# The last block of a convolutional MLP computed by feature tile in two banks, and a mean square issued between two products

## The reference

```python
mixed = jnp.sum(gates * proj, axis=2) @ w_out[l]
x = x + _rms_norm(mixed, norm_mix_post[l])
...                                   # cross attention: ox
x = x + _rms_norm(ox, norm_x_post[l])

hf = _rms_norm(x, norm_ffn_pre[l])
u = _dwconv_causal(hf @ w_up[l], ffn_dw[l]) + ffn_dw_b[l]
u_g, u_v = jnp.split(u, 2, axis=-1)
yff = (jax.nn.silu(u_g) * u_v) @ w_down[l]
x = x + _rms_norm(yff, norm_ffn_post[l])
```

## Time and profile before

| | |
|---|---|
| median of 3 runs | 1330.28 us (1328.29 to 1332.39) |
| the profiled execution | 1330.64 us |
| its span (first to last instruction) | 1328.5 us |
| PE busy | 1282.4 us (97%) |
| DVE busy | 838.8 us (63%) |
| ACT busy | 672.4 us (51%) |
| POOL busy | 57.7 us (4%) |
| granted TensorE clock, mean | 0.99 of full speed |
| read from HBM | 209.14 MB, 158 GB/s |

### The profile page before, as it was taken

How to read it: one execution, slowest core, us unless ns; L and a number is a source line. 1 busy time by engine, 2 the same in 40 slices (tenths; PEclk the granted TensorE clock), 3 DMA queues, 4 the chain that set the end, 5 groups by cost and what they waited for, 6 DMA issues and landing times.

```text
span 1328.5 us, 22392 instructions
## 1 busy us (share of the span) xinstructions
PE 1282.4 (97%) x9224; PEld 1201.5 (90%) x9224; DVE 838.8 (63%) x1129; ACT 672.4 (51%) x925; POOL 57.7 (4%) x101
## 2 busy tenths in 40 slices
PE   5999998999999999999999999899999998999997
PEld 5999997999999998899999999888999987999996
DVE  4874447655555655655555589986556566766664
ACT  4874656544445454444444554645354445654552
POOL 4000002000000000100000000010000010000000
PEclk8999999999999999999999999899999999999999
DMA  7750104555554644455654655444556642555550
GB/s 238 203 164 28 64 1 156 193 191 188 189 189 159 206 159 159 147 187 189 189 189 158 211 171 159 128 127 128 159 152 198 190 157 68 177 189 189 189 189 32
DMA packets 160465, 211.32 MB, mean 159 GB/s; under 512 B 5541, under 2 KB 143219, under 8 KB 160387
## 3 DMA queue, kind: packets, MB, share of 16 engines
q1 hardware_dynamic: 157299, 202.77, 48.0%
q0 software_dynamic: 2048, 7.37, 1.6%
q10 hardware_dynamic: 1040, 0.07, 0.1%
HBM read 209.14 MB, written 1.05 MB: 158 GB/s over the span
## 4 chain that ended last, share of the span: by engine, by line
PE 80%; DVE 11%; ACT 4%; issue 2%; DMA 2%; POOL 1%; DVEq 0%; SPq 0%; POOLq 0%; ACTq 0%
PE bank L306 23%; PE bank L309 23%; PE bank L310 23%; PE bank L1173 5%; DVE wlo L300 3%; DVE common L2198 2%; ACT whi L292 1%; PE bank L1662 1%; PE bank L1180 1%; ACT common L544 1%; DVE xlo L615 1%; DMA raw<-in_dn_w_in 1%; PE bank L2218 1%; PE bank L1744 1%; PE bank L1785 1%
## 5 line engine op out<-in xcount | busy, mean ns | idle before, releaser
L300 DVE TENSOR_TENSOR wlo<-raw,whi 128x2048 fp32r<-128x2048 f32 x191 | 437.1, 2291 | 248.4 <-ACT whi L292 248.0
L306 PE MATMUL bank<-xhi,whi 128*128 128x256 f32 x1824 | 523.5, 287 | 12.3 <-DVE xlo L615 11.4
L309 PE MATMUL bank<-xlo,whi 128*128 128x256 f32 x1824 | 516.9, 283 | 0.0
L310 PE MATMUL bank<-xhi,wlo 128*128 128x256 f32 x1824 | 516.9, 283 | 0.0
L292 ACT ACTIVATE whi<-raw 128x2048 fp32r<-128x2048 f32 x191 | 364.4, 1910 | 176.4 <-PE bank L306 107.2
L306 PEld LDWEIGHTS bank<-xhi,whi 128*128 128x128 f32 x1824 | 350.9, 192 | 18.1 <-issue 13.8
L309 PEld LDWEIGHTS bank<-xlo,whi 128*128 128x128 f32 x1824 | 350.8, 192 | 2.6 <-issue 1.0
L310 PEld LDWEIGHTS bank<-xhi,wlo 128*128 128x128 f32 x1824 | 350.6, 192 | 0.0
L306 PE MATMUL bank<-whi,hhi 128*128 128x512 f32 x392 | 154.0, 393 | 3.4 <-DVE hlo L2647 2.5
L309 PE MATMUL bank<-wlo,hhi 128*128 128x512 f32 x392 | 153.7, 392 | 0.0
L310 PE MATMUL bank<-whi,hlo 128*128 128x512 f32 x392 | 153.1, 390 | 0.0
(11 more groups left out here) (318 smaller groups left out, 1572.5 us busy)
## 6 DMA issues: line engine op xcount, KB each, us to landing
raw<-in_mlp_w_up SPq DMA_DIRECT2D x32, 1024.0 KB, 5.4
raw<-in_mlp_w_down SPq DMA_DIRECT2D x32, 1024.0 KB, 5.0
raw<-in_w_in SPq DMA_DIRECT2D x22, 1024.0 KB, 5.3
raw<-in_w_up SPq DMA_DIRECT2D x22, 1024.0 KB, 5.1
raw<-in_dn_w_in SPq DMA_DIRECT2D x16, 1024.0 KB, 6.1
raw<-in_w_gate SPq DMA_DIRECT2D x16, 1024.0 KB, 5.7
raw<-in_mb_w_in SPq DMA_DIRECT2D x12, 1024.0 KB, 5.1
raw<-in_w_down SPq DMA_DIRECT2D x11, 1024.0 KB, 4.8
```

The costliest lines, as they stand in the source:

```text
L300: nc.vector.tensor_tensor(wlo[:, s, :], raw[:, V % RAW, :], f32(whi[:, s, :]), ALU.subtract).then_inc(lo_ready, 1)
L306: ins = pe.matmul(o, shi, mhi, start=first, stop=False, skip_group_check=True)
L309: pe.matmul(o, shi, mlo, start=False, stop=False, skip_group_check=True)
L310: return pe.matmul(o, slo, mhi, start=False, stop=last, skip_group_check=True)
```

## The change

The last block (10) is computed differently from the other ten. Its gate half stays as it is. In its value half feature tile 0 goes to bank `G[1]` and feature tile 1 to bank `G[2]`, and each has its own signal when it is full. ScalarE applies silu ahead of the value half's first taps. First tap, other taps, product, `hhi` and `hlo` are then done for each feature tile on 256 columns. The order on ScalarE is first tap 0, first tap 1, `hhi` 0, `hhi` 1; on VectorE taps and product 0, taps and product 1, `hlo` 0, `hlo` 1. TensorE's last product waits for `hlo` 0 ahead of block 10's first feature tile (k = 0) and for `hlo` 1 ahead of its second (k = 1), in token tile 0 only. In `add_normed_rows` the mean square stands between the two products with the gains instead of behind them; this holds for all three places that use it.

```diff
-        def gemm_rows_by_tile(pe, Us, uses, operands, ready, first=False, between=None):
+        def gemm_rows_by_tile(pe, Us, uses, operands, ready, first=False, between=None, late=None):
...
                     for k in range(2):
+                        if late and t == 0 and n == len(Us) - 1:
+                            pe.wait_ge(late[k].sem, late[k].value)
                         for c in range(2):
...
                 for k in range(2):
                     use, squared = uses[2 * t + k], r.ss[2 * t + k]
+                    if k:
+                        dve_mean_square(dve, r, t)
                     dve.wait_ge(squared.sem, squared.value)
                     nc.vector.tensor_tensor(norm_x[:, t, HALF[k]], use.ps[:, :], gain_buf(g)[:, HALF[k]], ALU.mult)\
                         .then_inc(use.freed, 1)
-                dve_mean_square(dve, r, t)
...
+            z = tb[-1]
+            z_uses = [z.uses[1], G[2 + z.p].use() if z.p == 0 else G[0].use()]
+            z_y, z_mid, z_pr, z_hi, z_lo = (Signal(sem(f"ffn_last_{n_}")).many(2)
+                                            for n_ in ("first_tap", "mid", "prod", "hi", "lo"))
+            z_ft = z.ft + FF // P
+
+            def z_part(ap, f):
+                return ap[:, f * T:(f + 1) * T]
+
+            def pe_last(pe):
+                gemm_features(pe, z.us[0], z.uses[0], xhi, xlo)
+                sl_ = z.us[1] % RING
+                pe.wait_ge(lo_ready, z.us[1] + 1)
+                wh, wl = wview(whi, sl_, KT), wview(wlo, sl_, KT)
+                for f in range(2):
+                    if z_uses[f].n:
+                        pe.wait_ge(z_uses[f].freed, z_uses[f].n)
+                    fs = slice(f * P, (f + 1) * P)
+                    for k in range(KT):
+                        ins = mm3(pe, z_part(z_uses[f].ps, f), wh[:, k, fs], wl[:, k, fs], xhi[:, k, :], xlo[:, k, :],
+                                  k == 0, k == KT - 1, f == 0 and k == 0)
+                    ins.then_inc(z_uses[f].filled, 1)
+
+            def act_last(act):
+                act_half(act, z, 0, 0)
+                act_block(act, z, 0)
+                for f in range(2):
+                    act.wait_ge(z_uses[f].filled, z_uses[f].n + 1)
+                    nc.scalar.activation(z_part(cg[2 + z.p], f), z_part(z_uses[f].ps, f), ACT.Identity,
+                                         scale=w_ap(2, z_ft + f), bias=b_ap(z_ft + f)).then_inc(z_y[f].sem, 1)
+                for f in range(2):
+                    act.wait_ge(z_pr[f].sem, z_pr[f].value)
+                    nc.scalar.activation(hhi[:, z.p, f, :], z_part(prod[z.p], f), ACT.Copy).then_inc(z_hi[f].sem, 1)
+
+            def dve_last_taps(dve, f):
+                dve.wait_ge(z_y[f].sem, z_y[f].value)
+                dst = z_part(cg[2 + z.p], f)
+                for tap, sh in ((1, 1), (0, 2)):
+                    if tap == 0:
+                        dve.wait_ge(z_mid[f].sem, z_mid[f].value)
+                    ins = nc.vector.scalar_tensor_tensor(dst[:, sh:], z_part(z_uses[f].ps, f)[:, 0:T - sh],
+                                                         w_ap(tap, z_ft + f), dst[:, sh:], ALU.mult, ALU.add)
+                    ins.then_inc(z_mid[f].sem if tap else z_uses[f].freed, 1)
+                dve.wait_ge(z_uses[f].freed, z_uses[f].n + 1)
+                dve.wait_ge(z.sl.sem, z.sl.value)
+                nc.vector.tensor_tensor(z_part(prod[z.p], f), z_part(cg[z.p], f), dst, ALU.mult)\
+                    .then_inc(z_pr[f].sem, 1)
+
+            def dve_last_lo(dve, f):
+                dve.wait_ge(z_hi[f].sem, z_hi[f].value)
+                nc.vector.tensor_tensor(hlo[:, z.p, f, :], z_part(prod[z.p], f), f32(hhi[:, z.p, f, :]), ALU.subtract)\
+                    .then_inc(z_lo[f].sem, 1)
+
+            def dve_last(dve):
+                dve_half(dve, z, 0, 0)
+                dve_last_taps(dve, 0)
+                dve_last_taps(dve, 1)
+                dve_last_lo(dve, 0)
+                dve_last_lo(dve, 1)
...
                 gemm_rows_by_tile(pe, [td[-1], dl], acc, [(hhi[:, q], hlo[:, q]) for q in qs],
-                                  [[(prev[0], prev[1] + tail - 1)], [(prev[0], prev[1] + tail)]])
+                                  [[(prev[0], prev[1] + tail - 1)], []], late=z_lo)
```

More of the change, by code:

```diff
@@ L2700, in pe_f @@
                 for k in range(tail):
-                    pe_block(pe, tb[k])
+                    if k == tail - 1:
+                        pe_last(pe)
+                    else:
+                        pe_block(pe, tb[k])
                     q = (k + 1) % 2
@@ L2731, in act_f @@
                         act_all(act, lb[k], L[3 * k + 2], 12, i)
-                for k in range(tail):
+                for k in range(tail - 1):
                     act_all(act, tb[k], td[k], 0)
-                split_hi(act, dl)
+                act_last(act)
             def dve_f(dve):
@@ L2741, in dve_f @@
                         dve_all(dve, lb[k], L[3 * k + 2], 12, i)
-                for k in range(tail):
+                for k in range(tail - 1):
                     dve_all(dve, tb[k], td[k], 0)
-                split_lo(dve, dl)
+                dve_last(dve)
             return Part(pe=pe_f, act=act_f, dve=dve_f, acc=acc)
```

## The result

The changed kernel takes 1325.0 us (median of 5, 1323.55 to 1326.65), the kernel before 1332.16 us in the same comparison. The ratio is 0.995, with a 95% interval of 0.993 to 0.9969: between 4.1 and 9.3 us less, where 5.9 were forecast. The profiled execution took 1324.11 us, 6.5 less than the one before.

The account below looks back on a forecast made before the run. TensorE was taken to carry 80% of the chain, so less idle time or a shorter chain it waits for pays: 2.5 + 1.64 + 1.8 = 5.9 us less, 1324.3 us against the median, range 1322.3 to 1327.5.

Parts of the forecast that it names:

- The hole: TensorE's 2.62 us idle time between block 9's and block 10's rows in the last product: forecast to shrink by 2.5.
- Rival C: Last block: `hlo` of tile 0 comes late behind tile 1's product; hole 0.6 us, 1324.8 us; chance 0.05.
- rival E: Last block: the change doesn't take hold, tile 0's chain slides into tile 1's; 1325.8 us; chance 0.05.
- The clock: TensorE's matmuls behind the hole: without it no fall of the granted clock, 1.64 us less.
- rival A: Last product: TensorE's clock falls all the same, costing 1.64 us; 1326.0 us; chance 0.16.
- Rival D: Last product: without its hole TensorE stays at the low clock for all 48 matmuls; 1333.9 us; chance 0.04.
- The hand-overs and the tail: Behind mixer, cross attention and last product: earlier mean square gains 0.6 us in each hand-over, 0.62 in the tail.
- Rival B: Hand-overs and tail: POOL's root is blocked by VectorE's second product, taking 0.99 instead of 0.55; 1325.9 us; chance 0.08.
- one row of waits: Behind the hand-over's update, squares, root, transposes, split and TensorE's restart wait in a row, so the 0.6 gain is kept.
- low end: Whole kernel: upper bounds of all terms, 6.3 us, and 1.6 more should the clock's fall near 1104 vanish; 1322.3 us.
- the fall at 1104: TensorE's granted clock of 0.61 over 1104 to 1108; might vanish with the shifted hand-over, 1.6 us more gain.

Follow-up runs that it names:

- x8: Changed kernel, VectorE reordered: tile 1's update before tile 0's norm half in hand-overs, `hlo` 0 before product 1 in last block; ratio 0.9965 to kernel before.
- x10: Changed kernel with the last block's signals from existing semaphores and `hlo` of tile 0 ahead of tile 1's product; 1325.21 us, ratio 0.9951 to kernel before.
- x3: Kernel before, with ten spare TensorE products into an unused bank while it waits ahead of block 10; ratio 0.9984 to the kernel before.
- x5: Changed kernel with one bank for both feature tiles, signalled once, VectorE waiting for both first taps; ratio 0.9965 to the kernel before.
- x6: Kernel before, with an unused 512-column VectorE product beside POOL's root in the tail: one bank operand in tile 0, two buffers in tile 1; 1330.9 us.
- x1: Changed kernel with the mean square put back behind both products, so only the last block is changed; ratio 0.9968 to the kernel before.
- x7: Kernel before with only the last block's silu moved ahead of the value half's first taps on ScalarE; 1332.6 us, one run.
- x9: Kernel before with five more semaphores that nobody uses; 1331.05 us, one run.

## Why the prediction was right

**The hole.** Forecast 2.5 less (2.62 to 0.1); 2.62 to 0.00, with 0.08 in the first step behind it. The chain of small pieces was right to some hundredths: product and split at 0.42, `hlo` of tile 0 as the last thing to come, TensorE just at its own end when it comes. This is why x8's and x10's earlier `hlo` could gain only 0.08. Rival C needed small products and splits of 0.70, and they took 0.42; rival E needed tile 0's chain to slide into tile 1's, and tile 0's product ends at 1305.02, 0.91 before tile 1's taps begin.

**The clock.** Forecast 1.64 less; 9.66 - 8.02 = 1.64. That the hole is its cause was argued in the prediction from its place alone, and rival A stood against it; x3 shows it. In x5's one profile a hole of 1.8 us did no harm there. Rival D fell with the rows of the changed kernel: no matmul of the last product is at 0.43.

**The hand-overs and the tail.** Forecast 0.6 each and 0.62; they gave 0.63 and 0.64 (8.88 to 8.25 and 8.90 to 8.26) and 0.60. Rival B needed a root of 0.99 beside the second product; it took 0.55, and x6 shows both cases in one kernel. The prediction took all that stands behind the update as one row of waits; x8 shows a second path, that of tile 0's half. The change did not run into it, because that half keeps its place, 1.36 us behind the product before and after.

**The sum.** 2.62 + 1.64 + 0.63 + 0.64 + 0.60 = 6.13 us in the profile, forecast 5.9. One count in the prediction is off without touching the sum: ScalarE issues one instruction more, not two (its page has 926 beside 925, VectorE's 1131 beside 1129). The median came out at 1325.0 where 1324.3 was forecast, and the kernel before took 1.9 us more in this comparison than the median from which the forecast started. The timed gain of 4.1 to 9.3 us holds the forecast 5.9 but is too wide to test its terms; the rows do that. The profiled executions differ by 6.53; the rest is in places that the change doesn't touch: 1.56 less in the cross attention, where the clock did not fall this time, 1.05 more up to the first hand-over, 0.11 more behind the last update. The prediction's low end counted the fall at 1104 as something that a shorter hand-over might remove. It does not: x1 lacks the fall with the old hand-over, x5 and x8 have it with the new one. It comes and goes from profile to profile and is worth 1.3 to 1.6 us each time (31.15 to 31.43 beside 29.87). How much of the spread of the timed runs it makes up was not measured.

## What to carry to other kernels

Where the last chain behind a product decides when the next product starts, split it so that its first half runs under the producer's second half. Here smaller instructions with a wait for each tile, in one bank, took 0.8 of the 2.62 us and the second bank the rest; a list fitted to one bank was not tried. Price an idle hole of TensorE with the matmuls behind it: here a hole of 2.62 us cost 4.3. When a small GpSimd instruction is moved beside VectorE, look at the operands of what VectorE does then: with one from a bank the root kept its 0.55 here, with two buffers it took 0.38 to 0.44 us more. Whether that costs anything depends on what waits for the root: 0.38 in x6's tail, nothing in x8.

## What the runs showed of the hardware that I had not expected

Behind an idle time of 1.7 to 1.8 us in the last block the granted clock stayed at 1.00 (x5, one profile), and behind 2.5 to 2.6 seven or eight matmuls were at the low level (five profiles). The fall near 1104, behind idle times of 0.69 and 1.71 us, was there in seven of the twelve profiles (before, x3, x5, x6, x7, x8, x9) and missing in the other five, whatever was changed. The two idle times are the same in all twelve (0.69, then 1.70 or 1.71), so their length alone did not decide it. And with the code of the new last block the span was 0.5 us longer behind the last update while the device time hardly changed: a span is not the time that is measured.
